# Projections dealt out anew beside the attention of a two-layer hybrid decoder step: long token halves first, the second sample group's sum behind its scores, fewer constant matmuls

## The reference, cut to what matters

```python
z = x @ w_in                      # split: conv branch, q, k and v of three attentions, gates
conv_out = silu(layer_norm(depthwise_conv(glu(z)))) @ w_conv_out
o = gate0 * o_cmp + gate1 * o_slc + gate2 * o_win     # compressed, selected, window attention
attn_out = o @ w_attn_out
m = sigmoid(g_a) * conv_out + sigmoid(g_b) * attn_out
x = layer_norm(ALPHA * x + m @ w_o)
x = layer_norm(ALPHA * x + (silu(x @ w_gate) * (x @ w_up)) @ w_down)
```

## Time and profile before

| | |
|---|---|
| median of 3 runs | 1172.78 us (1170.25 to 1175.31) |
| profiled execution, its own time | 1173.74 us |
| its span, first to last instruction | 1171.9 us |
| granted TensorE clock, mean of the span | 0.973 |
| TensorE matmul busy | 1080.7 us, 92% |
| TensorE weight load busy | 1006.1 us, 86% |
| GpSimd busy | 768.8 us, 66% |
| VectorE busy | 550.4 us, 47% |
| ScalarE busy | 494.9 us, 42% |
| HBM, over the span | 157 GB/s |

### The profile page before, as it was taken

How to read it: one execution, slowest core, us unless ns; L and a number is a source line. 1 busy time by engine, 2 the same in 40 slices (tenths; PEclk the granted TensorE clock), 3 DMA queues, 4 the chain that set the end, 5 groups by cost and what they waited for, 6 DMA issues and landing times.

```text
span 1171.9 us, 24170 instructions
## 1 busy us (share of the span) xinstructions
PE 1080.7 (92%) x8062; PEld 1006.1 (86%) x8062; DVE 550.4 (47%) x1070; ACT 494.9 (42%) x902; POOL 768.8 (66%) x1077
## 2 busy tenths in 40 slices
PE   5998878988999999999989989889899999999996
PEld 5997747877898999999889968787788899999995
DVE  2998934535724222210159889553556322222003
ACT  4333345534436544433353233644244454444334
POOL 6998205433393989998549981354227479999882
PEclk9999888999999999999999897999999999999999
DMA  8656456641152665455256534775113335455541
GB/s 313 218 165 216 126 157 227 207 145 37 57 195 75 216 240 174 163 166 173 94 172 213 181 97 123 223 254 188 56 37 123 112 114 174 163 165 170 171 145 77
DMA packets 78146, 185.17 MB, mean 158 GB/s; under 512 B 9283, under 2 KB 42435, under 8 KB 77507
## 3 DMA queue, kind: packets, MB, share of 16 engines
q1 hardware_dynamic: 74130, 171.22, 44.3%
q10 hardware_dynamic: 3744, 11.40, 2.8%
q0 software_dynamic: 144, 0.96, 0.2%
HBM read 170.97 MB, written 12.57 MB: 157 GB/s over the span
## 4 chain that ended last, share of the span: by engine, by line
POOL 63%; issue 35%; POOLq 1%; DMA 1%; ACT 0%; SPq 0%
POOL w_lo L568 58%; POOL hid L591 3%; POOL res L589 2%; POOLq L562 0%; DMA wch<-weights_in 0%; DMA table<-page_table_in 0%; POOLq L586 0%; POOLq L148 0%; ACT w_hi L987 0%; POOL hid L589 0%; POOL hid L592 0%; SPq L430 0%; POOLq L574 0%; SPq L171 0%; POOLq L579 0%
## 5 line engine op out<-in xcount | busy, mean ns | idle before, releaser
L568 POOL TENSOR_TENSOR w_lo<-wch,w_hi 128x256 fp32r<-128x256 f32 x940 | 703.9, 782 | 391.9 <-ACT w_hi L987 390.1
L628 PE MATMUL proj<-x_hi,w_hi 128*128 128x288 f32 x1376 | 412.2, 300 | 25.2 <-POOL w_lo L568 17.3
L629 PE MATMUL proj<-x_hi,w_lo 128*128 128x288 f32 x1376 | 407.7, 296 | 0.0
L630 PE MATMUL proj<-x_lo,w_hi 128*128 128x288 f32 x1376 | 407.3, 296 | 0.0
L987 ACT ACTIVATE w_hi<-wch 128x1024 fp32r<-128x1024 f32 x235 | 248.3, 1057 | 225.5 <-PE proj L630 111.9
L628 PEld LDWEIGHTS proj<-x_hi,w_hi 128*128 128x128 f32 x1376 | 260.5, 189 | 38.1 <-issue 23.5
L629 PEld LDWEIGHTS proj<-x_hi,w_lo 128*128 128x128 f32 x1376 | 260.5, 189 | 0.0
L630 PEld LDWEIGHTS proj<-x_lo,w_hi 128*128 128x128 f32 x1376 | 260.4, 189 | 0.0
L1308 DVE SCALAR_TENSOR_TENSOR hid<-u_p,sm,hid 128x256 f32<-128x256 f32 x240 | 164.3, 755 | 3.4 <-DVE sq L1337 1.0
L646 PE MATMUL proj<-hid_lo,w_hi 128*128 128x288 f32 x352 | 104.2, 296 | 0.0
L644 PE MATMUL proj<-hid_hi,w_hi 128*128 128x288 f32 x352 | 103.8, 295 | 0.0
(11 more groups left out here) (240 smaller groups left out, 1340.1 us busy)
## 6 DMA issues: line engine op xcount, KB each, us to landing
wch<-weights_in SPq DMA_DIRECT2D x235, 512.0 KB, 3.3
pg<-cmp_pages_in SPq DMA_DIRECT2D x128, 128.0 KB, 2.8
pg<-slc_pages_in SPq DMA_DIRECT2D x128, 128.0 KB, 2.1
wn<-win_in SPq DMA_DIRECT2D x4, 2048.0 KB, 8.0
win_out<-wn ACTq DMA_DIRECT2D x4, 2048.0 KB, 8.7
hid<-w_in SPq DMA_DIRECT2D x2, 1024.0 KB, 5.6
kv_out<-kv ACTq DMA_DIRECT2D x2, 864.0 KB, 5.5
res<-xT_in SPq DMA_DIRECT2D x1, 1152.0 KB, 5.2
```

Source lines behind the costliest of these rows:

```text
L568: last = nc.gpsimd.tensor_tensor(lo[:, cols], raw[:, cols], hi[:, cols].bitcast(F32), ALU.subtract)
L628: mm(ps, hi[:, kb], x_hi[:, kb], start=kb == 0, stop=False)
L629: mm(ps, lo[:, kb], x_hi[:, kb], start=False, stop=False)
L630: last = mm(ps, hi[:, kb], x_lo[:, kb], start=False, stop=kb == KD - 1)
```

## The change

The program's text changes in four ways.

1. `unit_of` takes the place of `divmod`: the even units are now the second half of the tokens (long), the odd ones the first half (short). The head pairs keep their order.
2. The sum of the second group stands before its first fill, no longer behind it. The first group's sum stays behind two fills.
3. `FILLS` has a row for every piece. Units 1 and 3 have one fill and none (two each before), group 1 has three as before (now all of them of `w_in`), units 4, 5, 6, 7 have 3, 2, 3, 1 (2, 2, 1, 1 before). The sum is 22, as before.
4. `STEADY`: constant matmuls now before group 0 (9, none before), unit 1 (10, none), unit 3 (12, none), group 1 (9, 28 before) and unit 5 (12, 15 before); those before units 6 (9) and 7 (20) are gone. In sum 52 a layer, 72 before. The entries for `"second"` and `"norm"` stay.

```diff
-STEADY = {("second", 0): 20, ("second", 3): 16, ("g", 1): 28, ("u", 5): 15, ("u", 6): 9, ("u", 7): 20, "norm": 24}
+STEADY = {("second", 0): 20, ("second", 3): 16, ("g", 0): 9, ("u", 1): 10, ("u", 3): 12, ("g", 1): 9, ("u", 5): 12, "norm": 24}
 JOBS = [("g", 0)] + [("u", n) for n in range(4)] + [("g", 1)] + [("u", n) for n in range(4, 8)]
-FILLS = {("g", 0): (2, 2, 1), ("g", 1): (1, 1, 1), ("u", 6): (0, 0, 1), ("u", 7): (0, 0, 1)}
+FILLS = {("g", 0): (2, 2, 1), ("u", 0): (0, 1, 1), ("u", 1): (0, 0, 1), ("u", 2): (0, 1, 1), ("u", 3): (0, 0, 0), ("g", 1): (1, 1, 1),
+         ("u", 4): (0, 1, 2), ("u", 5): (0, 0, 2), ("u", 6): (0, 2, 1), ("u", 7): (0, 1, 0)}
+
+def unit_of(u):
+    return u // HALF, HALF - 1 - u % HALF
...
             def unit_scores(layer, u):
-                c, t = divmod(u, HALF)
+                c, t = unit_of(u)
...
                 for at, (kind, n) in enumerate(JOBS):
-                    fills = FILLS.get((kind, n), (0, 1, 1))
+                    fills = FILLS[kind, n]
+                    if kind == "g" and n:
+                        group_sum(layer, n)
                     for _f in range(fills[0]):
                         fill(layer)
-                    if kind == "g":
+                    if kind == "g" and not n:
                         group_sum(layer, n)
```

More of the change, by code:

```diff
@@ L758, in unit_transpose @@
             def unit_transpose(layer, u):
-                t = u % HALF
+                t = unit_of(u)[1]
                 keep_busy(STEADY.get(("u", u), 0))
```

## The result

The changed kernel takes 1167.34 us in the median of 12 runs (1160.79 to 1170.75), the one before 1173.16 us (12 runs, 1170.25 to 1177.25) beside it: ratio 0.994, interval 0.9925 to 0.9955. It is faster by 5.8 us, where 15 to 16 were forecast. Two later batches gave 0.9925 (0.9902 to 0.9949) for the same kernel and 0.9926 (0.9907 to 0.9945) for one that differs only in a load; with them the gain is 6 to 9 us.

What follows compares the result with a forecast made beforehand. TensorE was taken as the bound. Layer 0 saves 6.6 + 0.7 + 2.5 = 9.8 us, layer 1 6.6 + 0.7 - 0.5 = 6.8, together 16.6; less 1, 15.6 off 1173.74 gives 1158, range 1152 to 1167.

Steps and rivals of the forecast that it cites:

- Constants, 29 fewer, 6.6 us a layer: TensorE's queue outside the first group: 72 constant matmuls become 43 a layer, at 0.229 us each, 6.6 us less.
- Second group's sum: Attention, second group: sum ready 1.01 us behind the scores, its 8.4 us chain hidden by 8.8 of TensorE work, gap about 0.1.
- The gaps, 7.9 us: TensorE's idle gaps in a layer's attention part: 7.9 us in all against 8.6 before, 0.7 less.
- Units 0 and 4: TensorE's gaps before these units: 0.76 before unit 0, and unit 4's 2.05 shrinking to about that, counted as 0.8.
- Units 3 and 5: TensorE's gaps before these short units: 0.2 us each, with VectorE's scaling taken at 1.5 to 2.5 us.
- Unit 6: TensorE's gap before this long unit with a short one in front: taken as 0.2 us.
- The order of long and short units by itself costs nothing: Attention units: long ones still alternate with short ones and the sum of their work is the same, so no cost.
- The clock, 2.5 us: Layer 0, first group: nine constants before its transposes remove the clock fall behind them, saving 2.5 us once.
- Layer 1's cost of nine constants, 0.5: Layer 1, first group's transposes: 2.1 us of constants in a gap of 1.22, partly hidden by a later wait; cost 0.5.
- The 1 us at the ends: Allowance for small losses at the two layers' ends: 1 us taken off the 16.6 saved, leaving 15.6.
- The lock decides the gaps: Rival, chance 0.14: VectorE and GpSimd's shared-port lock adds 0.54 us at units 1, 2, 3, 5, 6, 7, 6.5 in all: 1164.6.
- The clock rivals: Two rivals: clock falls at each layer's end, 1165.4, chance 0.12; fewer constants let it fall at nine places, 1184, 0.04.

Runs made afterwards that it cites:

- no_constants: The changed kernel without its 52 constant matmuls a layer beside the attention units and groups; ratio to the kernel before 1.0087 (1.0069 to 1.0105).

## Why the prediction was wrong

Faster was right, at 0.88. The time, 1167.3 against 1158 and a range to 1167, was not: 5.8 us of 15.6 on record, 6 to 9 with the repeats. By its steps:

- **Constants, 29 fewer, 6.6 us a layer.** Right: they take 10.5 us now, 6.4 less.
- **Second group's sum.** Mechanism right (VectorE's wait 1.20, about 1 forecast), size off: gap 0.86 instead of 0.1, as the chain is 9.15 us from its first instruction to the end of its last (243.30 to 252.45), and by the same ends 8.32 in the earlier trace rows; two multiplies meet GpSimd. Without its work the chain is 8.32 here too, and the gap is gone.
- **The gaps, 7.9 us. This term failed**: they are 10.9 us, 3.0 more a layer, 6 in all, and 5.1 of the 10.9 go with GpSimd's work. Right within 0.15: units 1, 2, 7, the scores and unit 7's values. Wrong: the second group, above, and five units.
  - Units 0 and 4 are 1.25 each for 0.76 and 0.8. I carried over unit 0's gap of the earlier trace rows, where it was a short unit with one multiply lengthened. The long unit's scaling takes 3.6 us here (its large multiply alone 1.73), ahead of the copy of the group's rows. Without GpSimd's work the gap is 0.76 with the long unit too.
  - Units 3 and 5 are 0.78 and 0.61 for 0.2. Scaling a short unit "needs 1.5 to 2.5 us" was taken between its bounds; beside GpSimd it takes 3.0 from its first instruction. The trace of before had 2.8 already, at unit 4 (267.95 to 270.77).
  - Unit 6, a long one, is 0.69 for 0.2. VectorE starts to scale it when ScalarE's exponentials end, as at unit 1 in the earlier trace rows, and one multiply is lengthened by 0.54. The picture of 0.68 was the right one, and the 0.2 had no row behind it. Without GpSimd's work the gap is 0.15.
- **"The order of long and short units by itself costs nothing"**: wrong. It costs 12 us with the old fills, and the new fills with the old order cost 3. Only the pair pays.
- **The clock, 2.5 us.** The fall at 188 is gone, as said, and it was worth 2.3 us. But taking it away alone gave nothing, because the clock fell elsewhere. Layer 1, which had none before in three profiles, lost 1.6 or 1.7 in each of three after. Inside the attention parts layer 0 lost 2.5 us in the mean before and 0.2 after, layer 1 nothing before and 1.3 after: more than half of the saving counted in layer 0 was returned in layer 1. A clock level of 0.5 inside the attention part was also what the prediction named as a sign that it is wrong, and it shows at 300 and at 812 us.
- **Layer 1's cost of nine constants, 0.5**: nothing, in fact. From layer 1's first projection of x there to unit 0's scores it is 19.6 us in the mean of three profiles, before and after. The 1 us at the ends no run isolates.

So the sum closes: 6.6 for the constants, less 2.3 for the gaps (10.9 now, 8.6 before), is 4.3 a layer, and the attention parts without the clock's loss are 3.8 and 4.3 shorter; the clock gave back 2.3 in layer 0 and took 1.3 in layer 1. That is 9.1 us in the attention parts. The later batches show as much (8.7 and 8.8 by their ratios), the first one doesn't.

I had the mechanism that decides as a rival: "The lock decides the gaps" gave 1164.6, 0.54 us at each of six units. It gave the right sum, in part by luck, as its places were others (units 0 and 4 and the group are lengthened too; units 1, 2, 7 were as forecast). I weighed it at 0.14 because "my bounds of 1.5 to 2.5 hold most of it", and they did not. The clock rivals were half right: constants do hold the clock (no_constants), but with these 52 it falls only once or twice in the two attention parts.

What stays open: why the changed kernel's median was 1167.3 in one batch and 1164.4 and 1164.8 in two others of six runs. Stall and clock differ from one execution to the next by several us, and twelve runs leave the ratio open to 0.15% either way (the kernel of 1164.8 is the one with the cut load). No run tells how often the stall is long in either kernel.

## What to carry to other kernels

Where GpSimd works beside VectorE, cost every VectorE instruction on two SBUF inputs, and a multiply by a single number in SBUF, at its lengthened time (0.3 to 0.5 us more here), and count instructions rather than elements; copies and reductions kept their times here. A row of the same shape at a place without GpSimd is the wrong row. When a table of fills and an order of units change together, price the pair: a gap read before an edit belongs to the unit that stood there. Constant matmuls in a gap that another engine sets are free, and what they buy is a clock that stays up; a clock fall taken away at one place is no saving until several profiles show that it did not move to the next gap.

## What the runs showed that I had not expected

- The clock's falls come in pieces of about 1.5 and 3.3 us of lost time and change their place from one execution of the same kernel to the next: before lost 2.9 us at 188 to 196 in one profile and 1.6 at 236 to 242 in another. Gaps of 2.05 us had a fall behind them in one profile and not in others. At or behind each of the twelve gaps of 3.07 to 3.85 us in the attention parts of all profiles it fell, and so it did at the five stalls of 3.13 to 3.72 us near 420.
- A VectorE multiply of 128x2 takes 0.15 us alone and 0.69 beside GpSimd, one of 128x512 0.69 and 1.18: the addition is about the same. For the TENSOR_SCALAR of 128x544 it is 0.34.
- Idle time of VectorE's making can hold 6 us of additional matmuls a layer at no cost in time.
